# Mixture-of-experts tail of a three-layer model on one core: a fourth up-weight buffer, gathers ahead of the clears, transposed router logits, and combination joined with the last norm

## What is computed

```python
def hier_moe(h, w_rg, b_rg, w_re, b_re, w1e, w3e, w2e):
    t = h.reshape(-1, d)
    pg = jax.nn.softmax((t @ w_rg + b_rg).astype(f32), axis=-1)      # 4 groups
    pg_top, g_idx = lax.top_k(pg, 1)
    le = (t @ w_re + b_re).astype(f32).reshape(-1, N_GROUPS, EXPERTS_PER_GROUP)
    le_sel = jnp.take_along_axis(le, g_idx[:, :, None], axis=1)[:, 0]
    pe = jax.nn.softmax(le_sel, axis=-1)
    pe_top, e_idx = lax.top_k(pe, TOP_K)                             # 2 of 8
    pe_top = pe_top / jnp.sum(pe_top, axis=-1, keepdims=True)
    wts = pg_top * pe_top
    ...
    for e in range(N_EXPERTS):                                       # 32, 1024 -> 256 -> 1024
        he = jax.nn.silu(t @ w1e[e]) * (t @ w3e[e])
        out = out + cw[:, e:e + 1] * (he @ w2e[e])
...
        h2 = modulate(rmsnorm(x, g_ffn[l]), sh2, sc2)
        x = x + gt2[:, None, :] * hier_moe(h2, ...)
    return modulate(rmsnorm(x, g_final), shf, scf)
```

## Time and profile before

| | us |
|---|---|
| median of 3 runs | 2983.74 |
| lowest, highest | 2980.51, 2994.48 |
| profiled execution, its own time | 2988.74 |
| its span in the trace | 2986.4 |
| POOL's first clear in the expert stage | 2577.9 |
| first transposes of the expert stage | 2593.0 |
| first load of the combination | 2940.0 |
| first square of the last norm | 2963.5 |

### The profile page before, as it was taken

How to read it: one execution, slowest core, us unless ns; L and a number is a source line. 1 busy time by engine, 2 the same in 40 slices (tenths; PEclk the granted TensorE clock), 3 DMA queues, 4 the chain that set the end, 5 groups by cost and what they waited for, 6 DMA issues and landing times. The chain is left out here.

```text
span 2986.4 us, 37018 instructions
## 1 busy us (share of the span) xinstructions
PE 2567.0 (86%) x14214; PEld 1850.5 (62%) x14214; DVE 1245.8 (42%) x1586; ACT 958.0 (32%) x1334; POOL 980.1 (33%) x464
## 2 busy tenths in 40 slices
PE   8998898799897899789879989879877897589994
PEld 5776676588674666568658877567575685433331
DVE  5443624465544432362356654333645324311113
ACT  4542422445323232242244442244322323101112
POOL 5222322343475311142233437332121432223320
PEclk9999999899999898899989999889998898699996
DMA  3111222222363111122222226322001114499982
GB/s 119 64 43 57 99 71 85 70 85 98 116 224 124 43 48 37 49 92 85 64 77 98 93 104 221 117 72 75 2 3 45 66 61 157 166 361 341 329 317 93
DMA packets 73265, 333.77 MB, mean 112 GB/s; under 512 B 17177, under 2 KB 17177, under 8 KB 48793
## 3 DMA queue, kind: packets, MB, share of 16 engines
q1 hardware_dynamic: 59328, 313.98, 29.5%
q0 software_dynamic: 13824, 18.19, 1.8%
HBM read 372.67 MB, written 16.78 MB: 130 GB/s over the span
## 5 line engine op out<-in xcount | busy, mean ns | idle before, releaser
L495 POOL TENSOR_TENSOR dense_w_lo<-weights,dense_w_hi 128x1024 fp32r<-128x1024 f32 x84 | 203.5, 2425 | 470.5 <-ACT dense_w_hi L486 470.5
L220 PE MATMUL bank<-dense_s_hi,dense_w_hi 128*128 128x512 f32 x672 | 270.0, 402 | 65.7 <-DVE dense_s_lo L456 35.5
L222 PE MATMUL bank<-dense_s_hi,dense_w_lo 128*128 128x512 f32 x672 | 266.3, 396 | 0.0
L221 PE MATMUL bank<-dense_s_lo,dense_w_hi 128*128 128x512 f32 x672 | 266.2, 396 | 0.0
L486 ACT ACTIVATE dense_w_hi<-weights 128x1024 fp32r<-128x1024 f32 x84 | 88.9, 1058 | 345.7 <-PE bank L222 318.9
L220 PEld LDWEIGHTS bank<-dense_s_hi,dense_w_hi 128*128 128x128 f32 x672 | 129.5, 193 | 103.9 <-POOL dense_w_lo L495 38.9
L1245 DVE TENSOR_TENSOR hidden<-up_y 128x512 f32 x44 | 158.2, 3596 | 64.6 <-ACT up_y L1208 64.0
L222 PE MATMUL bank<-xn_r,weights_r 128*128 128x512 f32 x448 | 177.8, 397 | 0.0
L2712 PE MATMUL bank<-moe_weights,mix 128*64 128x512 f32 x504 | 172.6, 631 | 5.1 <-DMA moe_weights<-in_experts_up,moe_more_up 5.1
L220 PE MATMUL bank<-xn_r,mix_r 128*128 128x512 f32 x352 | 141.7, 403 | 38.0 <-DVEq L1233 38.0
L1586 DVE SCALAR_TENSOR_TENSOR xn<-mix,xn 128x1024 f32<-128x1024 f32 x64 | 118.1, 1846 | 123.6 <-DMA mix<-in_modulation 110.5
(11 more groups left out here) (623 smaller groups left out, 6049.7 us busy)
## 6 DMA issues: line engine op xcount, KB each, us to landing
weights<-in_w_up SPq DMA_DIRECT2D x44, 1024.0 KB, 4.9
weights<-in_experts_up SPq DMA_DIRECT2D x33, 1024.0 KB, 8.7
mix<-in_modulation SPq DMA_DIRECT2D x64, 512.0 KB, 4.7
moe_weights<-in_experts_up SPq DMA_DIRECT2D x31, 1024.0 KB, 11.0
weights<-in_w_xattn SPq DMA_DIRECT2D x24, 1024.0 KB, 4.9
weights<-in_w_down SPq DMA_DIRECT2D x44, 512.0 KB, 3.7
moe_weights<-in_experts_down SPq DMA_DIRECT2D x40, 512.0 KB, 8.1
weights<-in_w_attn SPq DMA_DIRECT2D x8, 1536.0 KB, 6.2
```

The costliest lines, as they stand in the source:

```text
L220: nc.tensor.matmul(out, left.hi, right.hi, start=first, stop=False)
L221: nc.tensor.matmul(out, left.hi, right.lo, start=False, stop=False)
L222: return nc.tensor.matmul(out, left.lo, right.hi, start=False, stop=last)
L495: nc.gpsimd.tensor_tensor(w[b].lo[:, :], units.rows(b, 0, D, 0, D), w[b].hi[:, :], ALU.subtract).then_inc(w_split, 1)
```

## The change

1. Router logits: the 36 router columns become the stationary weights and the 512 tokens are streamed, 8 matmuls instead of 32. The result is 36 x 512; ACT copies it to memory, and TensorE transposes it back by 4 small transposes behind the first token tile's rows. The table product alternates between even and odd tiles.
2. Experts: main up weights have four pairs of buffers; an up load waits for the step of expert e - 4. Four experts are loaded ahead in the router stage. The spare up weights get memory of their own.
3. POOL gathers first; only the two spare up buffers are cleared, after the first four gathers. (The fourth row buffer is now the memory of `std` and `rstd`, joined as `stds`.)
4. Combination and last norm are in the expert stage's block, by token tile: weigh and join in halves, transposes, add, square, mean, root, reciprocal, multiply (POOL, for the last tile VectorE), eight affine steps on ACT, and a store of 128 tokens.

```diff
-        self.main_ups = [ups[2 * i:2 * i + 2] for i in range(3)]
-        self.more_ups = ups[6:8]
+        self.main_ups = [ups[2 * i:2 * i + 2] for i in range(4)]
...
-            for e in range(3):
+            for e in range(4):
                 moe.load_up(sp, e)
                 moe.load_down(sp, e)
-            moe.load_down(sp, 3)
...
-            for t in range(TT):
-                for k in range(KT):
-                    mm = nc.tensor.matmul(g.bank[0][:, t * LOGITS:(t + 1) * LOGITS], g.xn[:, k, t * P:(t + 1) * P],
-                                          w_router[:, k * LOGITS:(k + 1) * LOGITS], start=(k == 0), stop=(k == KT - 1))
-            mm.then_inc(logits_done, 1)
+            for k in range(KT):
+                mm = nc.tensor.matmul(g.bank[6][0:LOGITS, :], w_router[:, k * LOGITS:(k + 1) * LOGITS], g.xn[:, k, :],
+                                      start=(k == 0), stop=(k == KT - 1))
+            mm.then_inc(logits_summed, 1)
...
+                if t == 0:
+                    pe.wait_ge(logits_read, 1)
+                    for j in range(TT):
+                        mm = nc.tensor.transpose(g.bank[0][:, j * LOGITS:(j + 1) * LOGITS], flat_logits[0:LOGITS, j * P:(j + 1) * P],
+                                                 g.ident[0:LOGITS, 0:LOGITS])
+                    mm.then_inc(logits_done, 1)
...
-            for h in range(2):
-                for n in range(2 * TT):
+            for n in range(2 * TT):
+                for h in range(2):
...
+            act.wait_ge(logits_summed, 1)
+            nc.scalar.activation(flat_logits[0:LOGITS, :], g.bank[6][0:LOGITS, :], ACT.Copy).then_inc(logits_read, 1)
...
-            for e in range(3, EXPERTS):
-                sp.wait_ge(up_done, main_step[e - 3] + 1)
+            for e in range(4, EXPERTS):
+                sp.wait_ge(up_done, main_step[e - 4] + 1)
                 moe.load_up(sp, e)
-                if e >= 4:
-                    sp.wait_ge(down_done, 2 * main_step[e - 4] + 2)
-                    moe.load_down(sp, e)
+                sp.wait_ge(down_done, 2 * main_step[e - 4] + 2)
+                moe.load_down(sp, e)
+            for b in range(2):
+                sp.wait_ge(scattered[b], 16 * STEPS // 2)
+            for t in range(TT):
+                sp.dma_start(pair_rows[t], pairs[t]).then_inc(loaded[t], 16)
+            for t in range(TT):
+                sp.wait_ge(final, t + 1)
+                sp.dma_start(out_ap[:, :, t * P:(t + 1) * P], g.mix[:, :, t * P:(t + 1) * P]).then_inc(stored, 16)
+            sp.wait_ge(stored, 16 * TT)
...
-            for here in rows:
-                nc.gpsimd.memset(here, 0.0).then_inc(cleared, 1)
-            for here in (*moe.more_ups, *moe.more_downs):
-                nc.gpsimd.memset(here, 0.0).then_inc(cleared, 1)
-            pool.wait_ge(cleared, len(rows) + 4)
             for n in range(ROWS_AHEAD):
                 gather(n)
+            for here in more_ups:
+                nc.gpsimd.memset(here, 0.0).then_inc(cleared, 1)
+            pool.wait_ge(cleared, 2)
             load_more_up(0)
...
+            for t in range(TT - 1):
+                pool.wait_ge(inverted, t + 1)
+                nc.gpsimd.tensor_tensor(y_of[t], x_of[t], inverse[t].unsqueeze(1).broadcast_to([P, KT, P]), ALU.mult).then_inc(scaled, 1)
...
+            turn_tile(0)
+            for t in range(TT):
+                if t + 1 < TT:
+                    turn_tile(t + 1)
+                mean(t)
...
+            weigh(0)
+            weigh(1)
+            for t in range(TT):
+                square(t)
+                if t + 2 < TT:
+                    weigh(t + 2)
+                root(t)
+                if t > 0:
+                    affine(t - 1)
+            affine(TT - 1)
...
+            join(0)
+            add(0)
             for t in range(TT):
+                if t + 1 < TT:
+                    join(t + 1)
+                    add(t + 1)
+                invert(t)
```

164 lines of the change are left out of this document (79 added, 85 removed).

## The result

| | before | after |
|---|---|---|
| median of the runs | 2984.4 us (2980.5 to 2994.5) | 2962.2 us (2961.2 to 2966.0) |
| span of the profiled execution | 2986.4 us | 2959.3 us |
| start of the router matmuls | 2537.0 | 2541.0 |
| from there to POOL's first work | 40.9 us | 40.6 us |
| POOL's first work to the first transposes | 15.1 us | 3.6 us |

The ratio is 0.9923, with a 95% interval of 0.9897 to 0.9949: 22 us less between the medians, 27.1 between the spans, against a forecast of 27.4. By the spans the total came out as forecast, by the medians 5 us short of it, and its terms did not come out: the expert stretch gained 17.6 us where 2 were expected, the tail lost 6.6 us where it was to gain 1.9, and the router gained 0.3 instead of 3.8. The rows ahead of 2541 belong to unchanged code.

A forecast was written before the change was run, and what follows sets the result against it. It took the expert stage to be held by eight TensorE waits, 26.6 us, on the single spare-tile buffer pair. Terms -3.8 - 11.5 - 2 - 8.2 - 1.9 = -27.4 us from 2983.74 gave 2956 us, range 2939 to 2972.

The forecast's parts named there:

- Part 1: Router logits: 8 streamed matmuls, a copy and small transposes instead of 32 matmuls, gaining 3.8 us.
- Part 2: Entry of the expert stage: gathers ahead of clearing start the first gather 11.5 us earlier, all of it gained.
- Part 3: Expert stage: a fourth main up buffer moves SP's issue times; value taken -2 us, bounds up to -19 us.
- rival (a): Expert stage: the fourth buffer empties the queue in time and later waits vanish, 17 us more, 2939 us; chance 0.10.
- 0.3 us for each of seven waits: Expert stage: the gain assumed for TensorE's waits for spare tiles with the fourth buffer, taken as -2 us.
- rival (c): Expert stage: SP's queue is never empty when POOL loads the spare tile, 16 us more, 2972 us; chance 0.10.
- (d): Expert stage: spare loads land still later, making a slower kernel; 3014 us at a 13 us landing; chance 0.04.
- signs of being wrong: TensorE waiting for a main expert's up weights, spare loads over 8 us, or the span ending with POOL's drain.
- Part 4: Seam behind the experts: no drain before the first load of pair rows, -8.2 us; the drain hidden at the end.
- Part 5: Combination and last norm by token tile: 44.5 us instead of 46.4, -1.9 us.
- rival (b): Tail by tiles is no gain: TensorE stays at 1.2 GHz, loop 8.5 us, tail 53, 2965 us; chance 0.15.
- the loop of 7.6 us: Tail: time per token tile at half clock, from reciprocal, half join, transposes, mean, root, semaphores and drain.

The follow-up runs named there:

- e8: The changed kernel with the router logits computed as before (32 matmuls with fresh weights): 2963.7 us, ratio 0.9935 to the kernel before.
- e11: The changed kernel with two spare pairs, one cleared in the router stage, a reordered tail and idle TensorE transposes: 2930.4 us, ratio 0.9820 to the kernel before.
- e3: The changed kernel with POOL's three multiplies of the last norm moved to VectorE: 2959.7 us, ratio 0.9923 to the kernel before.
- e4: The changed kernel with the old combination and last norm as stages of their own: 2964.7 us, ratio 0.9921 to the kernel before.
- e2: The changed kernel with three main up pairs, the fourth pair's memory given to the spare tiles: 2953.5 us, ratio 0.9876 to the kernel before.

## Why the prediction was right, point by point

**Sum.** Measured 2962.2, forecast 2956 us, range 2939 to 2972. The near hit in the difference of the spans (27.1 and 27.4 us) is chance: two large errors of opposite sign. The spans also hold 4 us by which the unchanged code ahead of the router differed. Taking the runs' group means for the expert stretch, the terms are -1.2 (router, by e8) +0.9 (POOL's start) -11.5 -11.3 -8.3 +6.6 = -24.8 us; the medians have 22, which fits the 6 to 9 us that the times give for the fourth pair.

**Part 1, router: -3.8 forecast, -1.2 found.** Its working for the logits was nearly right: they were ready 10.8 us after the first matmul, 3.2 earlier. The failed step is "the other 32 transposes ... run beside VectorE's routing arithmetic as before". The same transposes, at full clock and done early, left TensorE idle for 3.7 us, and the counting matmuls paid 2 us for the fallen clock (e11 gets them back). The bound that POOL begins when VectorE is done was also off: its first instruction was a clear that could start 0.3 us after the barrier, and is now an indirect DMA that starts 1.2 us after it, 0.9 us lost.

**Part 2, clearing: -11.5 forecast, -11.5 found**, no wait at `up(1)`, and the spare load at +9.5 and +10.8 us where +9.7 and +11.0 were counted.

**Part 3, fourth pair: -2 forecast, -11.3 found in the traces, -6 to -9 by the times.** The mechanism was named (only SP's moments of issue change, 3 MB ahead of POOL instead of 5) and so was rival (a) with the queue running empty, at a chance of 0.10. Mis-sized is the step "0.3 us for each of seven waits". It rested on "both leave about nothing to 3 us of queue". They are not alike: 2 MB less are 5 us of queue at the 400 to 430 GB/s of a full one, more than the 2 to 4 us that TensorE waited, and 3 us after POOL's issue the share is 0.03 to 0.15 in three of five cycles where it was 0.40 to 0.67 in four of five. The forecast should have spread its chance between -2 and -19, instead of taking the end next to zero. The Trainium skill's page "DMA: Bandwidth & Descriptors", section "Queues, rings and completion order", which speaks of engines that serve their queues in turn, was read there as an argument against the edit (rival (c)). The traces fit the rule, but it bears the other way: what counts is whether SP's queue is empty when POOL asks (shares of 0.03 to 0.15 against 0.39 to 0.54 above), and the fourth pair made it so more often. Rivals (c) and (d) did not come. Of the signs of being wrong one showed faintly: TensorE waited once for a main expert's up weights, for 0.25 us. Whether a spare load took over 8 us can't be said, as the trace of the kernel after has no landing times for them; in the kernel before some already did (up to 14.9 us, which the earlier trace rows don't show).

**Part 4, seam: -8.2 forecast, -8.3 found.** First load of pair rows 2.65 us after the scatter was issued. The drain at the end took 10.3 us instead of 7.9 and was hidden, with 7 us to spare.

**Part 5, tail: -1.9 forecast, +6.6 found**, which is rival (b)'s 53 us. Half of its condition came true. The forecast took 44.5 us, between 48.2 at half clock and 39 at full clock, and the clock did not pay: the means of the second tile ran at 0.50 throughout,

```profile
2927.28:2930.90 3.62, 3.62 (x17) 3.33 (x16) 1.20 (x5) 0.00 (x0) 0.00 (x0) 0.50 0.02 5
```

and those of the third and fourth at 0.50 and 0.52. So the 3.7 us taken off for the clock were the first part of the miss. Against the count at half clock the first root came earlier (+15.4 instead of +17.8 us), and the means paced as said (3.16 to 3.75 us). What failed there is the loop of 7.6 us. It was 9.3, 9.3 and 8.2, because "POOL's multiply has the whole loop for cover" is wrong: it runs beside VectorE's joins and makes them 2 us longer (e3). And the affine steps were put at 2.2 us a tile, between a quarter of the old 5.36 and the whole; they took 3.17, 0.39 us each, twice behind the last root and once in ScalarE's ring. From the last root to the end it was 10.8 instead of 7.6 us; the last store, put at 3 us, took 4.3 from the last affine step. Together: 3.7 (clock) - 2.4 + 4.0 (loops) + 3.2 (end) = 8.5 us, from 44.5 to 53.0. The old tail with its few large instructions was no worse (e4).

## What to carry to other kernels

Where a single buffer waits for a transfer of its own queue, give the next buffer to that one (e2), not to its neighbour, and clear it in a stage that has idle time. Before splitting a tail into tiles, write down each engine's queue in order and look for the rings: a step of tile t+1 behind a step of tile t-1 on one engine, and work of two engines on the same memory. And an engine that gets done earlier idles earlier: read the granted clock behind every gain on TensorE.
